# A two-layer encoder trunk in fp32r: head 0's value and gate products done plainly instead of with seven products

## The reference, cut to what matters

```python
def retention_layer(x, w_in, w_out, pos):
    h = x @ w_in                       # w_in: 1024 x 6144
    q, k, v, g = jnp.split(h, [D_MODEL, 2 * D_MODEL, 2 * D_MODEL + RET_WIDTH], axis=-1)
    # q, k: rope, 4 heads of 256;  v, g: 4 heads of 512
    # in each chunk: att = q k' * decay, inner = att v, cross = q state, state = decay * state + k' v
    # r = (inner + cross), normalized in each head of 512
    return (jax.nn.silu(g) * r) @ w_out
# x = post_norm(x, retention_layer(x));  shared k, v from x;
# x = post_norm(x, sliding_window_attention(x, k, v));  output x
```

## Time and profile before

| what | value |
|---|---|
| time, median of 3 runs | 2416.43 us (2411.99 to 2419.86) |
| profiled execution | 2416.58 us |
| its span | 2414.7 us |
| mean granted TensorE clock | 0.991 |
| DMA bytes | 443.38 MB, mean 184 GB/s |
| store of a set of sums (`t_prep<-t_buf`) | 28 of 1024 KB, 6.2 us to landing |
| load of half a set (`t_buf<-ret_w_in`) | 32 of 512 KB, 9.6 us |
| load of a pair of sums (`stage<-t_prep`) | 224 of 512 KB, 4.6 us |

### The profile page before, as it was taken

The page is one execution under the profiler, slowest core; times in us unless marked ns, Lnnn a source line. Parts: engine busy times, 40 slices in busy tenths (PEclk is TensorE's granted clock), DMA queues, the critical chain, the costliest instruction groups (busy, mean ns, idle before and its releaser), DMA issues.

```text
span 2414.7 us, 31064 instructions
## 1 busy us (share of the span) xinstructions
PE 2322.4 (96%) x11506; PEld 1889.5 (78%) x11506; DVE 1800.3 (75%) x2589; ACT 1193.0 (49%) x1777; POOL 340.7 (14%) x350
## 2 busy tenths in 40 slices
PE   6899889999999999999999999999999999999996
PEld 5677778777778888887777888888777888888775
DVE  7877878865886668884687766886478667788458
ACT  3433445347644445535754544553664445554463
POOL 4122111203001110111201011110210110011031
PEclk9999999999999999999999999999999999999998
DMA  9886676772764445754384544585257345454423
GB/s 328 283 300 251 237 235 228 243 261 71 236 209 149 132 130 173 258 162 147 104 286 134 175 149 132 166 276 183 71 169 258 115 139 166 122 189 152 122 79 122
DMA packets 215061, 443.38 MB, mean 184 GB/s; under 512 B 15040, under 2 KB 52432, under 8 KB 211328
## 3 DMA queue, kind: packets, MB, share of 16 engines
q1 hardware_dynamic: 200832, 375.58, 48.0%
q0 software_dynamic: 14080, 65.83, 7.4%
HBM read 379.75 MB, written 57.41 MB: 181 GB/s over the span
## 4 chain that ended last, share of the span: by engine, by line
PE 70%; DVE 15%; DMA 6%; issue 4%; ACT 3%; SPq 1%; POOL 0%; DVEq 0%; ACTq 0%; POOLq 0%
PE accs L663 19%; PE accs L665 18%; PE accs L664 18%; DVE w_lo L1319 4%; DMA stage<-t_prep 4%; PE bank L663 2%; PE bank L665 2%; PE bank L664 2%; PE bank L908 2%; ACT w_hi L990 2%; PE bank L917 1%; DMA stage<-ret_w_in 1%; PE bank L927 1%; PE bank L754 1%; DVE z L1630 1%
## 5 line engine op out<-in xcount | busy, mean ns | idle before, releaser
L1319 DVE TENSOR_TENSOR w_lo<-stage,w_hi 128x1024 fp32r<-128x1024 f32 x536 | 668.4, 1254 | 366.4 <-ACT w_hi L990 365.3
L990 ACT ACTIVATE w_hi<-stage 128x1024 fp32r<-128x1024 f32 x536 | 561.6, 1056 | 485.3 <-DMA stage<-t_prep 238.5
L663 PE MATMUL accs<-w_hi,xs 128*128 128x512 f32 x1120 | 447.0, 399 | 33.0 <-ACT sg L995 10.1
L665 PE MATMUL accs<-w_hi,xs 128*128 128x512 f32 x1120 | 440.2, 393 | 0.0
L664 PE MATMUL accs<-w_lo,xs 128*128 128x512 f32 x1120 | 439.6, 393 | 0.0
L663 PEld LDWEIGHTS accs<-w_hi,xs 128*128 128x128 f32 x1120 | 212.6, 190 | 83.6 <-issue 33.8
L665 PEld LDWEIGHTS accs<-w_hi,xs 128*128 128x128 f32 x1120 | 212.1, 189 | 45.6
L663 PE MATMUL accs<-x_hi,w_hi 128*128 128x512 f32 (+1 forms) x640 | 245.5, 384 | 1.2 <-ACT sgT L995 0.7
L664 PEld LDWEIGHTS accs<-w_lo,xs 128*128 128x128 f32 x1120 | 212.7, 190 | 42.3
L1980 POOL TENSOR_TENSOR rstd<-ve,half 128x1 f32<-128x1 f32 x96 | 79.4, 828 | 1178.0 <-DVE ve L1375 952.1
L664 PE MATMUL accs<-x_lo,w_hi 128*128 128x512 f32 (+1 forms) x640 | 237.5, 371 | 0.0
(11 more groups left out here) (199 smaller groups left out, 3828.0 us busy)
## 6 DMA issues: line engine op xcount, KB each, us to landing
stage<-t_prep SPq DMA_DIRECT2D x224, 512.0 KB, 4.6
stage<-ret_w_in SPq DMA_DIRECT2D x96, 512.0 KB, 4.0
stage<-ret_w_in SPq DMA_DIRECT2D x128, 256.0 KB, 3.0
stage<-swa_w_in SPq DMA_DIRECT2D x64, 512.0 KB, 4.0
t_prep<-t_buf POOLq DMA_DIRECT2D x28, 1024.0 KB, 6.2
stage<-ret_w_out SPq DMA_DIRECT2D x48, 512.0 KB, 3.7
cs<-rope_t SPq DMA_DIRECT2D x16, 1024.0 KB, 7.2
t_buf<-ret_w_in POOLq DMA_DIRECT2D x32, 512.0 KB, 9.6
```

The costliest lines, as they stand in the source:

```text
L663: mm(dst, lhs[0], rhs[0], start=start, stop=False, skip_group_check=reopened)
L665: return mm(dst, lhs[1], rhs[0], start=False, stop=stop, skip_group_check=reopened)
L990: copy(w_hi[:, g % HS], stage[:, g % LS], ACT.Copy).then_inc(w_hi_made, 1)
L1319: nc.vector.tensor_tensor(w_lo[:, g % LS], stage[:, g % LS], w_hi[:, g % HS].bitcast(F32), sub).then_inc(w_split, 1)
```

## The change

Head 0 of all four blocks makes v and gate with plain products: 8 pairs of raw weights (slots VG to VG + 7, `plain_vg_pair`), four for v and four for the gate, and each fills all four banks. The slots VG + 8 to VG + 13 of that head are vacant; the rings of weights count without them (`RING`, `ahead`, `before`). In that head ScalarE makes `v_hi` straight from the banks and VectorE `v_lo`, both at VG + 4; ScalarE makes `sg` with Silu from the banks after VG + 7. `score` moves to VG + 2 and `retain` to VG + 4, + 5, + 6.

Sets 0 to 3 are not made any more. The other sets have a new plan with a fifth buffer, which lies where `sg` and `gb` are. An entry is now set, buffer, block, slot of the load, slot of the first two additions (`begin_t`), slot of the last two (`end_t`).

VectorE makes the first sums of x instead of POOL, and they are split in slots 1 and 2. In the other heads some readings now stand ahead of `make_hi` or `make_lo`: `qr_hi` and `v_raw` at VG + 3, `after_retain` at VG + 11, and `split_x` at SO + 10 and SO + 12. `SUM_LOADS` has two loads later. A cache of split weights, which was empty and unused, is gone from the code.

```diff
+PLAIN = range(VG, VG + 8)
+VACANT = range(VG + 8, HEAD)
+PLAIN_BLOCKS = 4
...
+def vacant(g):
+    return g // NP < PLAIN_BLOCKS and g % NP in VACANT
+REAL = [g for g in range(NS * NP) if not vacant(g)]
+RING = {g: n for n, g in enumerate(REAL)}
...
+def ahead(g, n=AHEAD):
+    return REAL[RING[g] + n] if g in RING and RING[g] + n < len(REAL) else NS * NP
+def before(g, n):
+    return REAL[RING[g] - n] if RING[g] >= n else -1
+def plain(s, p):
+    return s < PLAIN_BLOCKS and p in PLAIN
+def plain_head(H):
+    return H % RH == 0 and H // RH < PLAIN_BLOCKS
...
-T_PLAN = [(0, 0, -1, 1), (1, 1, -1, 1), (2, 2, -1, 2), (3, 3, -1, 2), (4, 0, 8, 11), (5, 1, 9, 13), (6, 2, 10, 14),
-          (7, 3, 11, 16), (8, 0, 13, 17), (9, 1, 15, 20), (10, 2, 17, 20), (11, 3, 19, 21), (12, 1, 25, 31),
-          (13, 2, 28, 34), (14, 1, 35, 37), (15, 3, 30, 38), (16, 2, 37, 39), (17, 3, 42, 46), (18, 2, 45, 49),
-          (19, 3, 49, 52), (20, 2, 52, 55), (21, 3, 55, 57), (22, 3, 62, 65), (23, 3, 68, 70), (24, 0, 88, 100),
-          (25, 1, 88, 104), (26, 2, 100, 106), (27, 3, 100, 109)]
...
+T_PLAN = [(4, 4, 0, -1, 4, 4), (5, 0, 0, -1, 5, 5), (6, 1, 0, -1, 6, 6), (7, 2, 0, 1, 8, 8), (8, 3, 0, 2, 10, 10),
+          (9, 1, 0, 8, 11, 11), (10, 0, 0, 7, 18, 18), (11, 2, 0, 11, 19, 19), (12, 3, 0, 12, 20, 20), (13, 1, 0, 18, 21, 21),
+          (14, 2, 0, 22, 31, 31), (15, 1, 0, 25, 34, 34), (16, 3, 0, 23, 36, 36), (17, 2, 0, 35, 38, 38),
+          (18, 2, 0, 41, 47, 49), (19, 3, 0, 39, 52, 52), (20, 2, 0, 53, 55, 55), (21, 3, 0, 55, 57, 57),
+          (22, 3, 0, 61, 66, 66), (23, 3, 0, 70, 73, 73),
+          (24, 0, 0, 88, 100, 100), (25, 2, 0, 100, 104, 104), (26, 3, 0, 100, 106, 106), (27, 4, 0, 103, 109, 109)]
...
+def score_slot(H):
+    return VG + 2 if plain_head(H) else VG + 5
+def late_lo(H):
+    return () if plain_head(H) else (VG + 3, VG + 11)
+def retain_slots(H):
+    return (VG + 4, VG + 5, VG + 6) if plain_head(H) else (VG + 7, VG + 10, VG + 13)
...
-SUM_LOADS = {SO + 10: 1, SO + 12: 0, 1: 2, 3: 3}
+SUM_LOADS = {SO + 10: 1, SO + 12: 0, 6: 2, 9: 3}
...
+            if plain(s, p):
+                j, i = divmod(p - VG, 4)
+                return w_vg[:, i // 2, 2 * (i % 2):2 * (i % 2) + 2, j, 0, :]
...
-                if s == 0 and q in T_INDEX:
+                first_use = s == (PLAIN_BLOCKS if (kind, c) == ("vg", 0) else 0)
+                if first_use and q in T_INDEX:
...
+            def plain_vg_pair(s, p):
+                j, i = divmod(p - VG, 4)
+                wait_weights(s * NP + p)
+                for m in range(4):
+                    if i == 0:
+                        fill = VG + (4 * j if m < 2 else 2 + 4 * j)
+                        need(pe, acc_free[m], prior(s, fill, m))
+                    for u in range(2):
+                        k = 2 * i + u
+                        phys = m // 2 if k < 4 else (2, 6)[m // 2]
+                        cols = slice(m % 2 * P, (m % 2 + 1) * P)
+                        mm = mm3(acc[m], (xs[:, phys, 0, k % 4, cols], xs[:, phys, 1, k % 4, cols]), weights(s * NP + p, u),
+                                 k == 0, k == KD - 1)
+                    if m == 1:
+                        mm.then_inc(products, 1)
+                mm.then_inc(products, 1 if p < PLAIN[-1] else 1 + 2 * len(VACANT))
...
-                    if h < RH and j == VG + 5:
+                    if h < RH and j == score_slot(H):
                         score(H, 0)
-                    if h < RH and j in (VG + 7, VG + 10, VG + 13):
-                        t = (j - VG - 7) // 3
+                    if h < RH and j in retain_slots(H):
...
-                    hi_behind = h < RH - 1 and j == VG + 9 or p in (VG + 3, VG + 5, RO + 8, KV - 1, KV + 2, KV + 3, Q0 + 3)
+                    hi_behind = h < RH and (j == VG + 3 or h < RH - 1 and j == VG + 9) or p in (SO + 10, SO + 12, VG + 4 if plain(s, p) else VG + 5, RO + 8, KV - 1, KV + 2, KV + 3, Q0 + 3)
...
-                        if v == 4:
+                            make_hi(ahead(g))
+                        if v == 2 and plain_head(H):
+                            state_to_hi(H, 0)
+                        if v == 4 and plain_head(H):
+                            if s == 0:
+                                act.wait_ge(xs_split, 4)
+                            else:
+                                act.wait_ge(stored[0], 32 * s)
+                                act.wait_ge(stored[1], 32 * s)
+                                act.wait_ge(ln_dve, 8 * s)
+                            need(act, dstate_full, 8 * H)
+                            need(act, turned, 4 * H)
+                            act.wait_ge(products, used(s * NP + VG + 2) + 1)
+                            copy(v_hi[:, 0:2, :], accs[:, 0:2, :], ACT.Copy).then_inc(v_hi_made, 1)
+                            act.wait_ge(products, used(s * NP + VG + 3))
+                            copy(v_hi[:, 2:4, :], accs[:, 2:4, :], ACT.Copy).then_inc(v_hi_made, 1)
+                            make_hi(ahead(g))
+                        elif v == 4:
                             act.wait_ge(y_free, emptied(s, first_pair("vg", h, "P2"), 3))
...
+                            if v == 8:
+                                act.wait_ge(bias_copied, 1)
+                                if s == 0:
+                                    wait_stored(act, T_LAST_EARLY)
+                                need(act, gated, 4 * H)
+                                act.wait_ge(products, used(s * NP + VG + 6) + 1)
+                                copy(sg[:, 0:2, :], accs[:, 0:2, :], ACT.Silu).then_inc(x_free, 6)
+                                act.wait_ge(products, used(s * NP + VG + 7))
+                                copy(sg[:, 2:4, :], accs[:, 2:4, :], ACT.Silu).then_inc(y_free, 4)
...
+            def first_x_sums():
+                tt = nc.vector.tensor_tensor
+                tt(s3_tmp[:], x_part(0, 0, 0), x_part(0, 0, 1), sub).then_inc(x_summed, 1)
+                dve.wait_ge(x_summed, 1)
+                tt(s2_tmp[:], x_part(0, 1, 1), s3_tmp[:], sub).then_inc(x_summed, 1)
+                dve.wait_ge(x_summed, 2)
+                tt(x_part(0, 0, 0), s2_tmp[:], x_part(0, 0, 0), add).then_inc(x_summed, 1)
+                tt(x_part(0, 1, 0), x_part(0, 1, 0), s2_tmp[:], sub).then_inc(x_summed, 1)
...
-                    if first_step(p) is None and p not in (VG + 2, VG + 5, RO + 8, RO + 24, KV - 2, KV - 1, KV + 2, KV + 3, Q0 + 3)\
-                            and not score_first and p < SO:
-                        make_lo(g + AHEAD)
+                        make_lo(ahead(g))
+                    if first_step(p) is None and p not in (VG + 2, VG + 4 if plain(s, p) else VG + 5, RO + 8, RO + 24, KV - 2, KV - 1, KV + 2, KV + 3, Q0 + 3)\
+                            and not (score_first or h < RH and j in late_lo(H)) and p < SO:
...
+                        if not plain_head(H) and v == 3:
                             dve.wait_ge(products, full(s, p, 1))
                             dve.wait_ge(x_free, emptied(s, first_pair("vg", h, "P1"), 1))
                             nc.vector.tensor_tensor(v_raw[:, 0:2, :], v_raw[:, 0:2, :], accs[:, 2:4, :], add)\
                                 .then_inc(y_free, 2)
+                            make_lo(ahead(g))
...
+                        if plain_head(H) and v == 4:
+                            nc.vector.tensor_tensor(v_lo[:, 0:2, :], accs[:, 0:2, :], v_hi[:, 0:2, :].bitcast(F32),
+                                                    sub).then_inc(x_free, 2)
+                            dve.wait_ge(v_hi_made, 2 * H + 2)
+                            nc.vector.tensor_tensor(v_lo[:, 2:4, :], accs[:, 2:4, :], v_hi[:, 2:4, :].bitcast(F32),
+                                                    sub).then_inc(y_free, 2)
+                            make_lo(ahead(g))
...
+                        if not plain_head(H) and v == 11:
                             after_retain(H, 1)
+                            make_lo(ahead(g))
                             dve.wait_ge(v_hi_made, 2 * H + 2)
                             nc.vector.tensor_tensor(v_lo[:, 2:4, :], accs[:, 0:2, :], v_hi[:, 2:4, :].bitcast(F32),
                                                     sub).then_inc(x_free, 2)
...
+                    if p in (SO + 10, SO + 12):
+                        if s + 1 < NS:
+                            split_x(s + 1, (p - SO - 10) // 2)
+                        make_lo(ahead(g))
+                    for n, _, in_block, _, begin, end in T_PLAN:
+                        if (in_block, begin) == (s, p):
+                            begin_t(n)
+                        if (in_block, end) == (s, p):
+                            end_t(n)
```

More of the change, by code:

```diff
@@ L268, in build @@
         G = reserve(8 * KB)
+        t_buf = [at(f"t_buf{i}", [P, 2, 2, 512], off)
+                 for i, off in enumerate((R, R + 8 * KB, R + 16 * KB, R + 24 * KB, G))]
         sg = at("sg", [P, NT, RV], G)
@@ L983, in make_hi @@
             def make_hi(g):
```

(15 more changed lines are left out.)

286 lines of the change are left out of this document (128 added, 158 removed).

## The result

The changed kernel takes 2396.63 us, median of 4 runs (2393.78 to 2398.44), against 2415.97 for the kernel before, also of 4, on the same chip (2411.99 to 2419.86): a ratio of 0.9919, 95% interval 0.9899 to 0.9939. It is faster by more than the 0.3% that can be told, and 1.6 us from the forecast of 2395. The profiled execution has a span of 2396.0 us against 2414.7: 18.7 us less, where 21.3 were forecast.

What follows compares the result with a forecast made beforehand. TensorE, busy for 96% of the span, was taken as the bound. Block 0 gains 37.2 us, the others pay 15.9, so -21.3: from 2416.6 to 2395 us, own range 2384 to 2408 (chance 0.70), 8-in-10 range 2382 to 2413.

Steps and rivals of the forecast that it cites:

- What should show it: 96 more matmuls, w_hi 512 times; head 0 takes 82 to 87 us in block 0, about 82.4 in the others.
- Part 1: Head 0 of every block: 24 more matmuls at 0.227 us, 5.4 us each; blocks 1 to 3 pay 15.9 altogether.
- The hand-overs in the plain head: Head 0, blocks 1 to 3: TensorE waits 0.7 us for krT behind qk pairs, 0.5 for v_lo at VG+4.
- att_lo's 1.3 us: Head 0, blocks 1 to 3: wait of 1.3 us for att_lo goes, as first score comes 10.9 us ahead of retention.
- Part 2: Sets 0 to 3 are never made, so head 0 of block 0 falls to 84.2 us, 15.2 us less.
- Part 3: New set plan and reading order: block 0's heads 1 to 3 and rest change by -9.8, -5.4, -5.8, -1.0 us.
- 3 us in head 1: Block 0, head 1: 3 us left over block 1's pace, against 12.8 before, so 9.8 us gained.
- Late w_hi: Block 0, heads 1 to 3: sets 8 to 13 stored several pairs ahead, so late w_hi (36.5 us ScalarE idle) goes.
- the 2.4 us for rT: Block 0, head 3: 2.4 of the 5 us left stays for rT, as set 20 is made no sooner.
- first rival: Block 0 stays late: heads 1 to 3 and the rest keep all 38.9 us, 2417 us, no change; chance 0.13.
- second: Head 0's bank hand-over at VG + 4 is in series, 9.2 us each: 2430 us, slower; chance 0.09.
- third: Nothing is left of block 0's excess, the 17 us left in the sum gone: 2378 us; chance 0.08.

Runs made afterwards that it cites:

- experiment 2: Changed kernel with the old order of readings set back (plain head and new set plan kept): 2409.35 us, ratio 0.9968.
- experiment 4: Changed kernel with the plain head in block 0 alone, sets 0 to 3 made late in block 0: 2407.93 us, ratio 0.9970.
- experiment 1: Kernel before with the new order of readings alone, seven products in head 0 and all 28 sets kept: 2403.20 us, ratio 0.9949.
- experiment 6: Changed kernel with st_lo made behind both v_lo in the plain heads: 2395.17 us, ratio 0.9905.
- Experiment 5: Changed kernel with the previous block's last LayerNorm step moved behind krT in VectorE's queue, blocks 1 to 3: 2391.83 us, ratio 0.9885.
- experiment 3: Changed kernel with make_hi and make_lo ahead of the x splits again at SO + 10 and SO + 12: 2395.20 us, ratio 0.9916.
- experiment 7: Changed kernel with the bias table written at slot 60 of block 0 instead of slot 30: 2399.16 us, ratio 0.9924.
- experiment 8: Changed kernel with the bias table written at slot 60 and sets 14 to 16 loaded later: 2398.02 us, ratio 0.9918.
- experiment 11: Changed kernel with plain head 0 in blocks 0 and 1 alone, sets 0 to 3 made late in block 1: 2391.37 us, ratio 0.9889.
- experiment 9: Changed kernel with the last LayerNorm step behind krT and the bias table written at slot 36 instead of 30: 2387.86 us, ratio 0.9866.
- experiment 10: Changed kernel with the last LayerNorm step behind krT, bias write at slot 36 and st_lo behind both v_lo: 2387.64 us, ratio 0.9862.
- experiment 12: Changed kernel with the four sums of the first x tile on GpSimd again instead of VectorE: 2400.56 us, ratio 0.9913.

## Why the prediction was right, point by point

**What should show it.** The counts are as forecast: w_hi 512 times, each line of additions on `t_buf` 24 times, 96 matmuls more; head 0 of block 0 lies within 82 to 87 us, and head 0 of blocks 1 to 3, forecast at about 82.4, takes 83.7, 81.4 and 82.2. Of the 11 us that were left to heads 1 to 3 of block 0, 13.3 came, 9.5 of them in head 1.

**Part 1, the price of plain products.** The matmuls stand. There are 96 more, and in the plain pairs of block 1 they start as far apart as in a qk pair; these two are 28 steps apart, 0.227 us each:

```profile
654.68 0.39 PE L693 MATMUL accs<-w_lo,xs 128*128 128x512 f32 x1
...
661.03 0.39 PE L694 MATMUL accs<-w_hi,xs 128*128 128x512 f32 x1
```

For the 72 matmuls of blocks 1 to 3 this pitch makes 16.3 us. The 131 ns that the Trainium skill gives in a stream ("TensorE: Matmul & The Clock Gate", section "Back-to-back issue gap") would make 9.4, and the trace doesn't agree with it. What the plain heads cost these blocks as a whole depends on the order of readings. With the old one they got 12.2 us longer (kernel before to experiment 2). With the new one the answer is 17.1 (experiment 4) or 22.4 (experiment 1 to the changed kernel). The two differ because experiment 4 has waits for att_lo of 1.8, 2.1 and 2.8 us in its blocks 1 to 3 that experiment 1 has not; which of its other differences brings them was not tried. The forecast was 15.9, and the change as a whole made blocks 1 to 3 longer by 6.4, 4.4 and 1.4 us, 12.2.

**The hand-overs in the plain head.** v_lo: 0.5 us forecast, 0.5 measured, and experiment 6 shows that it was for VectorE's queue, as argued. krT: 0.7 forecast with an upper bound of 1.2; 1.9, 1.2 and 1.2 measured, so above the bound in block 1. The term was worked out with the old order, and there it holds: in experiment 2 the waits for krT are 0.2, 0 and 0 us, with z at 1.8, 1.4 and 2.7. The new order takes the wait for z away, so TensorE is at the end of the qk pairs sooner and VectorE, with its four LayerNorm steps, is not: krT ends 4.8 us behind them instead of 3.4, and 4.8 less the 2.9 us of the half pair is the 1.9 that was measured. The prediction moved the readings, but left z's wait as it was and worked krT's out from rows with the old order. Experiment 5, which moves one LayerNorm step, settles it. att_lo's 1.3 us went, as forecast, but the order alone does that (experiment 1), not only the longer way from score to retention.

What came back against krT's excess is the wait for z (5.4 us in blocks 1 to 3 before, 1.5 after) and 0.2 to 0.4 us in each of heads 1 and 2. Experiment 2 makes the same 12 us without the new order, so the order is not why the total stays under 15.9. That difference of 3.7 us is no larger than the spread between profiles of the same code, and its cause stays open.

**Part 2, head 0 of block 0.** 84.2 us forecast, 85.1 measured (82.7 to 84.1 in experiments 3, 5, 7, 8 and 11, with the same head). krT's 7.3 us went; qrT kept 2.4 (1.5 forecast, bounds 0 and 5), v_lo 1.5. The timeline of ScalarE shows what is in front of qrT, a w_hi whose load from the raw weights was late, as argued:

```profile
34.26 1.06 ACT L1043 ACTIVATE w_hi<-stage 128x1024 fp32r<-128x1024 f32 x1 [5.75 <-DMA stage<-ret_w_in]
35.23 1.00 ACT L1209 ACTIVATE qrT<-accs 128x1024 f32<-128x1024 f32 x1
```

**Part 3, heads 1 to 3 and the rest.** Here the sizes were off, in both directions. Head 1 was forecast at 80.1 us and took 86.6: the step "3 us in head 1" is the mis-sized term, by 6.5 us. Late w_hi did not go: ScalarE is idle for stage loads from `t_prep` for 31.1 us in heads 1 to 3, where it was 36.5. Of the excess, 2 to 4 us are the write of the bias table, which the prediction never looked at (experiments 7 to 10). What is left, 83.0 us in experiment 9 against 78.1 in block 1, which has 1.4 us of matmuls more, stays: the pairs take a median of 9.9 us to land there even without the write. The loads of sets 14 to 16 have a part in that, but taking them away only moved the wait to sg (experiment 8); what the stores of sets do was not tried. Head 2 was forecast at 80.1 and took 78.9, head 3 at 82.9 and took 79.9: the 2.4 us for rT that I left there went. The prediction had tied them to set 20, rightly, but that set's store landed 2.8 us faster than before (experiment 2), which it didn't foresee. The rest of the block took 278.9, not 275.6: the late sets are in it, with a wait for `vs<-vcar` that grew from 1.8 to 3.4 us (experiment 11).

**The sum.** Block 0 gave -30.7 for -37.2, the others +12.2 for +15.9: -18.5 for -21.3. Inside block 0 the errors are +0.9, +6.5, -1.2, -3.0 and +3.3 us for the four heads and the rest. So part of the agreement is luck: errors of 6.5 us in block 0 and 3.7 in the others had opposite signs, and the forecast was nearer than its terms. The mechanism held where most of the gain was placed: head 0 of block 0 is 14.3 us shorter for 15.2. What part of these the sets that are not made have, apart from the new plan of the others, was not tried; the sums of x on VectorE have some 3 us (experiment 12).

**The rivals.** Block 0 did not stay late as a whole (first rival, 2417 us): of its 38.9 us in heads 1 to 3 and the rest, 3.3 + 6.6 + 8.8 - 2.3 = 16.4 went, where the forecast had 22.0. Without the new order it would have been closer: 2409 us. The hand-over is not in series (second, 2430 us; its sign, over 3 us for v_lo or v_hi in head 0 of block 1, is 0.5). Something is left of block 0's excess (third, 2378 us), and experiment 9 takes another 4.5 us of it (604.9 for 609.4), with 6.8 us of blocks 1 to 3 (585.8, 586.0, 598.8).

## What to carry to other kernels

A wait of TensorE names the reading that came last, not what made it late: an edit that reorders one queue often moves the same lateness to the next reading (experiment 3), so price the lateness of the engine and not the wait. When work is taken out of a crowded stretch, look at everything else that is issued there, a small one-off write included, and put it where no late loads stand; then check the stretch it went to. And when a cost is moved to another stage, count the sharing of buffers there: four sets more made late in block 0, in buffers that qT needed, cost 33 us, and the same ones made late in block 1, where there are no others, cost 4 to 7.
